# Weight chunks split into a high and a low part: the low part written over the raw chunk, eight slots for each, and unsplit chunks left out

## The reference

```python
h = rms_norm(x, norm_mix[layer])
(a_q, ..., merge_gate) = jnp.split(h @ w_in[layer], SPLIT_POINTS, axis=-1)
```

## Time and profile before

| | us |
|---|---|
| median of 3 runs | 3404.14 |
| lowest, highest | 3403.9, 3407.31 |
| profiled execution, its own time | 3407.14 |
| its span, first to last instruction | 3405.4 |
| TensorE busy in the span | 3291.9 |
| VectorE busy | 1948.1 |
| ScalarE busy | 1664.9 |
| GpSimd busy | 184.7 |
| mean granted TensorE clock | 0.987 of 2.4 GHz |

### The profile page before, as it was taken

The page is one execution under the profiler, slowest core; times in us unless marked ns, Lnnn a source line. Parts: engine busy times, 40 slices in busy tenths (PEclk is TensorE's granted clock), DMA queues, the critical chain, the costliest instruction groups (busy, mean ns, idle before and its releaser), DMA issues.

```text
span 3405.4 us, 41414 instructions
## 1 busy us (share of the span) xinstructions
PE 3291.9 (97%) x15346; PEld 2737.7 (80%) x15346; DVE 1948.1 (57%) x2331; ACT 1664.9 (49%) x2256; POOL 184.7 (5%) x199
## 2 busy tenths in 40 slices
PE   8999999999999999999999899999989798999998
PEld 7888778888888888888877788888878677888886
DVE  5566545555555555556555666556655656664665
ACT  5555544444444444445444455445545645553553
POOL 0023100000000000001001100000000011000001
PEclk9999999999999999999999999999989899999999
DMA  8845556666666666655565556566554544656653
GB/s 258 235 140 154 165 177 193 189 185 193 187 190 191 188 184 190 192 175 172 153 192 159 183 162 185 190 187 184 185 159 127 169 138 161 184 188 195 184 180 131
DMA packets 324437, 608.82 MB, mean 179 GB/s; under 512 B 19468, under 2 KB 46424, under 8 KB 323632
## 3 DMA queue, kind: packets, MB, share of 16 engines
q1 hardware_dynamic: 320768, 594.05, 56.7%
q0 software_dynamic: 3504, 12.52, 1.3%
HBM read 603.22 MB, written 3.28 MB: 178 GB/s over the span
## 4 chain that ended last, share of the span: by engine, by line
PE 94%; DVE 2%; ACT 1%; issue 1%; DMA 0%; POOL 0%; SPq 0%; DVEq 0%; ACTq 0%
PE ps L302 29%; PE ps L304 29%; PE ps L303 29%; PE ps L341 2%; PE ps L444 1%; PE ps L468 1%; ACT w_hi L271 1%; DVE w_lo L277 0%; PE ps L433 0%; POOL main L834 0%; PE ps L470 0%; DVE xres L1859 0%; DVE stats L1566 0%; PE ps L446 0%; PE ps L914 0%
## 5 line engine op out<-in xcount | busy, mean ns | idle before, releaser
L277 DVE TENSOR_TENSOR w_lo<-raw,w_hi 128x1024 fp32r<-128x1024 f32 (+1 forms) x1142 | 1420.7, 1252 | 1244.3 <-ACT w_hi L271 1239.3
L271 ACT ACTIVATE w_hi<-raw 128x1024 fp32r<-128x1024 f32 (+1 forms) x1142 | 1197.0, 1054 | 1509.3 <-PE ps L304 1472.8
L302 PE MATMUL ps<-w_hi,l_hi 128*128 128x512 f32 (+2 forms) x2848 | 1113.4, 391 | 14.0 <-issue 6.4
L303 PE MATMUL ps<-w_lo,l_hi 128*128 128x512 f32 (+2 forms) x2848 | 1098.9, 386 | 1.5 <-issue 1.5
L304 PE MATMUL ps<-w_hi,l_lo 128*128 128x512 f32 (+2 forms) x2848 | 1099.3, 386 | 0.0
L302 PEld LDWEIGHTS ps<-w_hi,l_hi 128*128 128x128 f32 x2848 | 538.0, 189 | 121.7 <-issue 10.8
L302 PE MATMUL ps<-w_hi,m_hi 128*128 128x512 f32 (+1 forms) x1600 | 624.0, 390 | 10.4 <-DVE main L1883 5.5
L304 PEld LDWEIGHTS ps<-w_hi,l_lo 128*128 128x128 f32 x2848 | 537.7, 189 | 107.0
L303 PEld LDWEIGHTS ps<-w_lo,l_hi 128*128 128x128 f32 x2848 | 538.5, 189 | 102.1 <-issue 1.9
L304 PE MATMUL ps<-w_hi,m_lo 128*128 128x512 f32 (+1 forms) x1600 | 620.0, 387 | 0.0
L303 PE MATMUL ps<-w_lo,m_hi 128*128 128x512 f32 (+1 forms) x1600 | 619.9, 387 | 0.0
(11 more groups left out here) (293 smaller groups left out, 1544.0 us busy)
## 6 DMA issues: line engine op xcount, KB each, us to landing
raw<-ffn_up SPq DMA_DIRECT2D x256, 512.0 KB, 4.1
raw<-w_in SPq DMA_DIRECT2D x176, 512.0 KB, 3.7
raw<-w_mlp_in SPq DMA_DIRECT2D x128, 512.0 KB, 3.8
raw<-w_mlp_out SPq DMA_DIRECT2D x128, 512.0 KB, 3.9
raw<-ffn_down SPq DMA_DIRECT2D x128, 512.0 KB, 4.6
raw<-ab_w_in SPq DMA_DIRECT2D x64, 512.0 KB, 3.8
raw<-w_branch SPq DMA_DIRECT2D x48, 512.0 KB, 3.9
raw<-cd_w_in SPq DMA_DIRECT2D x40, 512.0 KB, 4.3
```

Source lines behind the costliest of these rows:

```text
L271: nc.scalar.activation(w_hi[:, k % SPLIT, 0:n], raw[:, k % RING, 0:n], ACT.Copy).then_inc(hi_done, 1)
L277: nc.vector.tensor_tensor(w_lo[:, k % SPLIT, 0:n], raw[:, k % RING, 0:n], w_hi[:, k % SPLIT, 0:n].bitcast(F32), ALU.subtract).then_inc(lo_ ...
L302: nc.tensor.matmul(o, xh, hi[:, j, :], start=first and j == 0, stop=False)
L303: nc.tensor.matmul(o, xh, lo[:, j, :], start=False, stop=False)
```

## The change

`raw` and `w_lo` now lie in the same bytes: a tensor `raw` is declared, its space given back, and `w_lo` with eight slots is put there. `w_hi` has eight slots as well, so the total is the same 64 KB a partition (before 8 + 4 + 4 slots, now 8 + 8). The low split writes its result over the raw chunk that it reads. A load waits for `chunk_used` of chunk k-8 in place of `lo_done`. The high split has no wait for a free slot of its own any more. A table `WIDTH` gives the width of every chunk outside loops: narrow chunks are split over their own width, and the two chunks of pooling weights and the two of LRU weights have width 0 and are not split; the semaphores are counted up for them. The places of the splits in the engines' programs stay.

```diff
-        raw = sb("raw", [P, RING, CHUNK])
-        w_hi = sb("w_hi", [P, SPLIT, CHUNK], F32R)
-        w_lo = sb("w_lo", [P, SPLIT, CHUNK], F32R)
+        raw_guard = nc.sbuf_tensor("raw", [P, RING, CHUNK], F32)
+        raw = raw_guard.__enter__()
+        raw_guard.__exit__(None, None, None)
+        w_lo = sb("w_lo", [P, RING, CHUNK], F32R)
+        w_hi = sb("w_hi", [P, RING, CHUNK], F32R)
...
-            wait(sp, lo_done, 8 * q + k - RING + 1)
+            wait(sp, chunk_used, 8 * q + k - RING + 1)
...
+        def width(q, k):
+
+            return WIDTH.get(8 * q + k, CHUNK) if isinstance(q, int) else CHUNK
+
+        def split_hi(act, q, ks):
 
             for k in ks:
+                n = width(q, k)
                 wait(act, raw_in[k % RING], 16 * (q + k // RING + 1))
-                wait(act, chunk_used, 8 * q + k - SPLIT + 1)
-                nc.scalar.activation(w_hi[:, k % SPLIT, 0:n], raw[:, k % RING, 0:n], ACT.Copy).then_inc(hi_done, 1)
+                if n == 0:
+                    act.wait_ge(hi_done, 8 * q + k)
+                    act.sem_inc(hi_done, 1)
+                    continue
+                nc.scalar.activation(w_hi[:, k % RING, 0:n], raw[:, k % RING, 0:n], ACT.Copy).then_inc(hi_done, 1)
+
+        def split_lo(dve, q, ks):
 
             for k in ks:
+                n = width(q, k)
                 dve.wait_ge(hi_done, 8 * q + k + 1)
-                nc.vector.tensor_tensor(w_lo[:, k % SPLIT, 0:n], raw[:, k % RING, 0:n], w_hi[:, k % SPLIT, 0:n].bitcast(F32),
+                if n == 0:
+                    dve.wait_ge(lo_done, 8 * q + k)
+                    dve.sem_inc(lo_done, 1)
+                    continue
+                nc.vector.tensor_tensor(w_lo[:, k % RING, 0:n], raw[:, k % RING, 0:n], w_hi[:, k % RING, 0:n].bitcast(F32),
                                         ALU.subtract).then_inc(lo_done, 1)
...
+        WIDTH = {k: 2 * A_BLOCKS[b][1] for k, (b, c) in enumerate(A_ORDER) if b is not None}
+        WIDTH.update({8 * Q_AB + 8 * b + c: 2 * AB_TAIL for b in range(3) for c in range(NCH)})
+        WIDTH.update({8 * (Q_CD + 5) + O4 + c: 2 * CD_BLOCKS[5][1] for c in range(NCH)})
+        WIDTH.update({8 * (Q_AB + AB_POOL) + x: 0 for x in range(2)})
+        WIDTH.update({8 * (Q_CD + CD_LRU) + O2 + x: 0 for x in range(2)})
```

More of the change, by code:

```diff
@@ L297, in mm_chunk @@
+            lo = w_lo[:, k % RING, 0:len(kts) * w].rearrange("p (a b) -> p a b", b=w)
             for j, kt in enumerate(kts):
@@ L906, in cmp_chunk @@
                 pe.wait_ge(lo_done, k + 1)
-                whi = w_hi[:, k % SPLIT, :].rearrange("p (a b) -> p a b", a=4)
-                wlo = w_lo[:, k % SPLIT, :].rearrange("p (a b) -> p a b", a=4)
+                whi = w_hi[:, k % RING, :].rearrange("p (a b) -> p a b", a=4)
+                wlo = w_lo[:, k % RING, :].rearrange("p (a b) -> p a b", a=4)
                 o = ps[0:30, 4 + s, 0:256]
@@ L1242, in rows_a @@
                 scaled(b, b, A_END[b], lambda tt: zA[:, tt, c:c + w], ST["rstd"], b % 2, w=w)
-            split_hi_a(act, 8, A_END[0] + SPLIT)
+            split_hi(act, 0, range(8, A_END[0] + SPLIT))
             rows_a(0)
-            split_hi_a(act, A_END[0] + SPLIT, A_END[1])
+            split_hi(act, 0, range(A_END[0] + SPLIT, A_END[1]))
             act.wait_ge(cw_ready, 1)
@@ L1252, in _ @@
             i.then_inc(thi_done, 1)
-            split_hi_a(act, A_END[1], A_END[1] + SPLIT)
+            split_hi(act, 0, range(A_END[1], A_END[1] + SPLIT))
             rows_a(1)
-            split_hi_a(act, A_END[1] + SPLIT, A_END[1] + SPLIT + 2)
+            split_hi(act, 0, range(A_END[1] + SPLIT, A_END[1] + SPLIT + 2))
             act.wait_ge(sp_v, 1)
             nc.scalar.activation(sp_e, sp_t, ACT.Exp).then_inc(sp_a, 1)
-            split_hi_a(act, A_END[1] + SPLIT + 2, A_END[2] + SPLIT)
+            split_hi(act, 0, range(A_END[1] + SPLIT + 2, A_END[2] + SPLIT))
             rows_a(2)
-            split_hi_a(act, A_END[2] + SPLIT, A_END[3] + SPLIT)
+            split_hi(act, 0, range(A_END[2] + SPLIT, A_END[3] + SPLIT))
             rows_a(3)
-            split_hi_a(act, A_END[3] + SPLIT, A_END[4] + SPLIT)
+            split_hi(act, 0, range(A_END[3] + SPLIT, A_END[4] + SPLIT))
             rows_a(4)
@@ L1265, in _ @@
             nc.scalar.activation(hgr.rearrange("p (s h) -> p s h", s=2), ps[0:30, 4:6, 0:256], ACT.Gelu_apprx_tanh).then_inc(cmp_gelu, 1)
-            split_hi_a(act, A_END[4] + SPLIT, A_END[4] + SPLIT + 2)
+            split_hi(act, 0, range(A_END[4] + SPLIT, A_END[4] + SPLIT + 2))
             act.wait_ge(cmp_pe, 1)
             nc.scalar.activation(hg.rearrange("p a b c -> p (a b c)"), ps[:, 4, 0:120], ACT.Copy).then_inc(cmp_gelu, 1)
-            split_hi_a(act, A_END[4] + SPLIT + 2, A_END[5] + SPLIT)
+            split_hi(act, 0, range(A_END[4] + SPLIT + 2, A_END[5] + SPLIT))
             act.wait_ge(chunk_used, A_END[5])
@@ L1610, in _ @@
             inverse(0, ST["rstd"], ST["root"])
-            split_lo_a(dve, 8, A_END[0] + SPLIT + 2)
+            split_lo(dve, 0, range(8, A_END[0] + SPLIT + 2))
             dve.wait_ge(small_in, 16 * N_SMALL)
             windows()
-            split_lo_a(dve, A_END[0] + SPLIT + 2, A_END[1])
+            split_lo(dve, 0, range(A_END[0] + SPLIT + 2, A_END[1]))
             windows_lo()
-            split_lo_a(dve, A_END[1], A_END[1] + SPLIT)
+            split_lo(dve, 0, range(A_END[1], A_END[1] + SPLIT))
             softplus_in()
-            split_lo_a(dve, A_END[1] + SPLIT, A_END[2])
+            split_lo(dve, 0, range(A_END[1] + SPLIT, A_END[2]))
             dve.wait_ge(sp_a, 1)
@@ L1629, in _ @@
             nc.vector.tensor_scalar(decay, sp_t, -8.0, None, ALU.mult)
-            split_lo_a(dve, A_END[2], A_END[3] + SPLIT + 2)
+            split_lo(dve, 0, range(A_END[2], A_END[3] + SPLIT + 2))
             bias_rows()
-            split_lo_a(dve, A_END[3] + SPLIT + 2, A_END[5] + 2)
+            split_lo(dve, 0, range(A_END[3] + SPLIT + 2, A_END[5] + 2))
             dve.wait_ge(cmp_pe, 2)
@@ L1635, in _ @@
             nc.vector.tensor_copy(vc[0:N_CMP, :, :], ps[0:N_CMP, 6:8, 0:P]).then_inc(cmp_done, 1)
-            split_lo_a(dve, A_END[5] + 2, A_END[5] + SPLIT)
+            split_lo(dve, 0, range(A_END[5] + 2, A_END[5] + SPLIT))
             dve.wait_ge(acc_free, 6)
```

5 lines of the change are left out of this document (1 added, 4 removed).

## The result

The changed kernel runs in 3383.25 us (median of 4 runs, 3379.58 to 3385.66), the kernel before, beside it, in 3404.89 us (4 runs, 3403.9 to 3407.31): ratio 0.9934, interval [0.9917, 0.9952], that is 16 to 28 us faster. Forecast: 3382.5, range 3373 to 3396. The profiled execution took 3382.36 us, span 3379.8, mean clock 0.990.

What follows compares the result with a forecast made beforehand. TensorE, busy 3291.9 of 3405.4 us, was taken as the bound. Terms summed to 21.7 us, giving 3385.4 against the profiled execution and 3382.5 us for the median; range 3377 to 3390, with rivals A and B 3373 to 3396.

Steps and rivals of the forecast that it cites:

- Barriers: Three barriers before a new x: the last addition starts 2.2 us sooner at each, 6.7 us in all.
- rival B: Clock gives back more: six stretches behind gaps, partly at 1.2 GHz, lose low-clock time; 3374 us, chance 0.14.
- End of the MLP: Last product of the MLP: the addition no longer follows a throttled high split, 2.2 us gained.
- Index step: TensorE's 6.67 us wait at L1063: the pooling branch's high split starts sooner, 2.2 us; bounds 0 to 6.67.
- Pooling product: Gap of 1.61 us at L1048, its chain behind one high split of 1.06 us: 0.9 us gained.
- Mixer: Start of the mixer: gap falls from 2.41 to 1.4 us, 1.0 us, plus 1.6 us from the clock behind it.
- Merges: Four merges where TensorE waits 0.6 us each for GpSimd's sum: product comes 2.2 us sooner, 2.5 us in all.
- LRU stretch: LRU and up-projection: 0.9 us at the gate product, 2.2 from narrower splits, 1.5 at a later gap; 4.6 us.
- The later loads: Loads issued later keep 12.7 us of slack, 5.2 us in the narrowest chunks: cost 0.
- Rival C: Slower: low splits ready sooner hold up GpSimd's scaling in 56 attention units; about 3410 us, chance 0.06.
- Rival A: Gaps are handed on: the next wait is nearly as late; only about 10 us gained, 3394 us, chance 0.12.
- D: Splits run no further ahead because loads hold them; only the widths' 2 us gained, 3402 us, chance 0.06.

Runs made afterwards that it cites:

- run 3: The kernel before with only the width table added, narrow chunks being split over their own width: 3403.42 us, ratio 0.9998.
- run 4: The changed kernel with the slot wait put back only for the last four high splits ahead of the three barriers: 3391.34 us, ratio 0.996.
- run 1: The changed kernel with one wait put back: a high split waits again until chunk k-4 is used up. 3407.75 us, ratio 1.0009.
- run 2: The kernel before with only the late loads: a load waits until chunk k-8 is used up, not for its low split. 3409.3 us, ratio 1.0013.
- run 5: The changed kernel with the position bias rows stored 16 times in place of 32 and read back in twice as many transfers: 3386.17 us.
- run 6: The changed kernel with the position bias rows stored 64 times in place of 32 and read back in half as many transfers: 3391.69 us.
- run 9: The changed kernel with GpSimd's bias store split: 8 heads' rows and one copy before the first attention, the rest after chunk 68 is used: 3383.87 us.
- run 10: The changed kernel with GpSimd's bias store split and the first attention's bias reads held until chunk 60 is used: 3380.0 us.
- run 12: The changed kernel with the split bias store, first attention's reads held until chunk 60 is used, and 30 filler matmuls in each barrier gap: 3373.28 us, ratio 0.9904.
- run 8: The changed kernel with bias rows stored 16 times in place of 32 and 24 filler matmuls in each of the three barrier gaps: 3383.11 us.
- run 11: The changed kernel with 30 matmuls that feed nothing in each of the three barrier gaps: 3376.5 us.

## Why the prediction was right, and where its errors cancelled

*Barriers: 6.7 forecast; 6.8 us of gap (3 x 2.28), 8.5 with the clock (7.3 against run 3).* The mechanism and the starting point (addition within 0.1 us of the last matmul) are as forecast; run 4 shows the price by itself, 8.1 us. What was left out of the step is the clock behind the restart. It was rival B, of which less than half came true, here and by 1.1 us in the LRU stretch.

*End of the MLP: 2.2 forecast, 2.25 (3.37 to 1.12).* Against run 3 it is 3.2: behind this gap the clock is at 1.2 GHz for 3.4 us in the traces of runs 1 to 3, and not in those of the kernel before and the changed one. *Index step: 2.2, 2.28 (6.67 to 4.39). Pooling product: 0.9, 1.0.* The whole block gave 2.9 (3.5 against run 3) for the forecast 3.1.

*Mixer: 1.0 + 1.6 forecast, 2.6 by the chunks. The 1.0 is shown, the 1.6 was luck.* The gap is 1.40, and the window behind it reads a clock of 1.00:

```profile
1831.00:1835.00 4.00, 4.00 (x23) 3.40 (x24) 0.00 (x0) 1.85 (x4) 0.00 (x0) 1.00 0.31 120
```

But run 3, with the old gap of 2.41 us ahead of it, reads the same, where the earlier trace rows have 0.60:

```profile
1838.80:1842.80 4.00, 4.00 (x23) 3.38 (x22) 0.00 (x0) 1.58 (x3) 0.00 (x0) 1.00 0.42 134
```

Runs 1 and 2 have that gap and no low clock there either. The half clock behind it was one profile's own, and I had taken its price as the change's to give back. Against run 3 the start of the mixer gains 1.0 us, the gap alone.

*Merges: 2.5, all four gaps gone.* One low split did go ahead of GpSimd's addition, as the rule of the Trainium skill (SBUF — State Buffer, "Who interferes with whom") had it: GpSimd's 2.39 us became 3.31, the two low splits take 4.55 together where one free of GpSimd takes 1.23, and the 2.2 us cover it.

*LRU stretch: 4.6 forecast, 7.7 by the chunks, 5.1 against run 3. Here a term was wrong in its cause.* I gave 2.2 us to the narrower splits on a ScalarE "without a pause". Runs 2 and 3 give them nothing: as soon as a split gets shorter it meets its wait for TensorE. Run 1 has the widths and no run-ahead, and gaps of 2.94 and 3.88; the changed kernel has 1.04 and 2.92. The run-ahead is thus worth 2.9 us there in a kernel with the narrow splits. Whether they have a part in it is open, as no run has the run-ahead without them. I had put a saving on an engine beside the wait that eats it. The other terms came: 1.0 at L1178 for 0.9, and 1.6 us (4.27 to 2.65) for 1.5 at the gap behind the rotations, though the gap after it grew by 0.25. All gaps of the stretch together are 6.5 us shorter than in the profile before. The 1.1 left of the 7.7 goes with the clock, at 1.2 GHz for 23.9 us of the stretch in the profile before and for 17.1 after.

*The later loads: 0 forecast, 2.3 us in the profile, 4.4 in run 2. This is the step that failed.* The text had the condition: "the price starts only where a landing is 5 us longer". In the changed kernel, chunk 55's load is issued at 131.53 and lands 9.8 us later, 6.4 over the 3.4 of the earlier trace rows. Less the lead of 5.2 us that is 1.2 us, and TensorE's gap there is 1.17 us: the sum was sound, its landing was not. That 3.4 is a median over all sixteen loads of the kind, and I used it for a stretch in which GpSimd moves 2.7 MB of its own. Before, the same chunk's load went out at 122.69, ahead of GpSimd's store, and landed after 3.5 us. Here is the DMA traffic of 125 to 165 us, changed kernel (share of 16 engines is the last column):

```profile
q1 hardware_dynamic: 5611, 7.66, 61.7%
q0 software_dynamic: 880, 2.75, 30.0%
...
bias_rows<-late POOLq DMA_DIRECT2D x1, 1152.0 KB, 10.7
main<-bias_rows POOLq DMA_DIRECT2D x4, 256.0 KB, 7.6
```

The two queues together take 92% of the DMA engines' time there. Runs 5, 6, 9 and 10 settle that GpSimd's transfers are the cause.

*The total.* Forecast 21.7 us of terms; by the two profiles 25.6 of span, 20.0 against run 3, and 21.6 by the medians. Against run 3 the gain falls short of the forecast by 2.5 us before chunk 62, 1.6 at the mixer and 0.9 at the loop edge, and exceeds it by 1.0 at the end of the MLP, 0.7 each at the merges and the barriers, 0.5 in the LRU stretch and 0.4 in the pooling and index block. So the mechanism, the run-ahead, was right and most of its places came as sized, but that the total met the median within 1 us is luck: a missed cost and a clock term that was not the change's stood against several gains that were a little too small, and the interval of the result is 12 us wide. *Rival C* did not come: GpSimd's piece in attention takes 0.93 and 0.60 us as before, and between chunk 65 and the first merge the difference of the two kernels does not grow. *Rival A* is refuted by the gaps, *D* by run 1, where all of the gain goes with the run-ahead.

Open is the clock's scatter. Behind the 3.49 us gap at 433 us it is at 1.2 GHz in the trace of run 12 and not in that of run 10, with the same code there. It makes 1.5 us between the traces of run 10 and the changed kernel. So single profiles differ by a microsecond or two in a stage that no edit explains, and run 3 can't be told by its time from the kernel before, nor run 9 from the changed one.

## What to carry to other kernels

A wait for a free slot, in an in-order queue, costs nothing on its own engine and everything to the instruction behind it: look for gaps of the bound engine whose chain has a throttled instruction in front, count them, and expect its duration back from each. When a change moves a load's issue nearer to its use, read the landing in the narrowest stage at its own time, with what other queues move then, and not the median of the kernel. A saving on an engine that is throttled by a wait is worth nothing while the wait stands. And when a term of a forecast rests on the clock behind one gap of one profile, look at that place in a second profile first.

## What was not expected of the hardware

A load of 268 KB, 3.4 us by the median, took 9.8 us beside a 1.18 MB store of GpSimd's, and up to 15.1 us (run 8) beside sixteen of its reads. Filling 6.96 of 7.0 us of idle TensorE with matmuls that feed nothing made the kernel faster by 6.75 us in the medians (run 11). By the chunks of its profile 4.5 us of that lie at the three barriers (1.0, 2.8 and 0.6); the rest is not placed, and may be the scatter of four runs against four. At the first and the third barrier the clock was still at 1.2 GHz for 3.4 us, at the second not at all, though all three have the same 1.89 us gap behind the transposes. So that gap alone does not explain it, and what does is open.
